# Two transformer layers with routed experts: TensorE's expert pairs written out, and loads and products of the second layer placed beside its attention's end

## The reference, cut to what matters

```python
mp = jnp.split(cond_ctx @ mod_w[layer] + mod_b[layer], N_MOD, axis=-1)
...
xs = xs + ms[2][:, None, :] * ys
...
aff = jax.nn.softmax(jnp.dot(xt, w_router), axis=-1)
g, idx = lax.top_k(aff.T, cap)
xe = xt[idx]
h = jax.nn.silu(xe @ w_gate) * (xe @ w_up)
ye = (h @ w_down) * g[..., None]
out = jnp.zeros_like(xt).at[idx.reshape(-1)].add(ye.reshape(-1, D))
```

## Time and profile before

| | |
|---|---|
| median of 3 runs | 1890.08 us (1889.51 to 1894.63) |
| the profiled execution's own time | 1888.88 us |
| its span in the profile | 1886.9 us |
| TensorE matmul busy | 1660.1 us, 88% of the span |
| VectorE, ScalarE, GpSimd busy | 602.3, 364.8, 312.2 us |
| data moved | 525.07 MB, mean 278 GB/s |
| mean granted TensorE clock | 0.948 |

### The profile page before, as it was taken

One profiled execution on the slowest core, in us unless ns is written; L12 is line 12 of the kernel. 1 busy time (PEld: TensorE's weight loads), 2 busy tenths in 40 slices (PEclk: granted clock), 3 DMA queues, 4 the chain that ended last, 5 costly groups with the idle time before them and its releaser, 6 DMA issues.

```text
span 1886.9 us, 30470 instructions
## 1 busy us (share of the span) xinstructions
PE 1660.1 (88%) x13255; PEld 771.5 (41%) x13255; DVE 602.3 (32%) x1077; ACT 364.8 (19%) x725; POOL 312.2 (17%) x358
## 2 busy tenths in 40 slices
PE   4799868479999999999989788893899999999997
PEld 0688546123332322332258666562233233233322
DVE  2568564510110110120176577535101101210102
ACT  2377731100000000000052365402000000000000
POOL 1133230110101110110020167301101101101110
PEclk8899979789999999999989899896899999999999
DMA  9400642989999999999830201019799999999993
GB/s 391 139 1 1 246 167 112 414 328 407 379 409 375 392 406 371 385 406 413 333 137 1 95 24 33 36 44 417 268 395 391 405 366 388 407 373 391 411 358 116
DMA packets 57682, 525.07 MB, mean 278 GB/s; under 512 B 12351, under 2 KB 12639, under 8 KB 24782
## 3 DMA queue, kind: packets, MB, share of 16 engines
q1 hardware_dynamic: 47968, 490.62, 64.5%
q0 software_dynamic: 8176, 27.08, 5.3%
q10 hardware_dynamic: 1406, 5.38, 0.7%
HBM read 500.50 MB, written 22.55 MB: 277 GB/s over the span
## 4 chain that ended last, share of the span: by engine, by line
PE 77%; DVE 10%; DMA 5%; ACT 4%; issue 3%; POOL 1%; SPq 0%; DVEq 0%; POOLq 0%; ACTq 0%
PE ps L862 36%; PE ps L866 17%; PE ps L813 6%; PE ps L1104 4%; DMA W<-x_hat,gi_c 2%; DMA ring<-in_mod_w 2%; DMA ring<-in_rg_w_in 1%; PE ps L1152 1%; PE ps L1139 1%; PE ps L1126 1%; PE ps L889 1%; PE ps L1024 1%; PE ps L904 1%; ACT W L1332 1%; PE ps L1002 1%
## 5 line engine op out<-in xcount | busy, mean ns | idle before, releaser
L862 PE MATMUL ps<-ring,W 128*32 128x512 f32 x4608 | 558.4, 603 | 19.3 <-issue 18.0
L866 PE MATMUL ps<-ring,W 128*16 128x512 f32 x2304 | 300.6, 594 | 0.0
L862 PEld LDWEIGHTS ps<-ring,W 128*32 128x32 f32 x4608 | 146.8, 111 | 353.3 <-issue 351.1
L1172 ACT ACTIVATE W<-ps 128x512 f32<-128x512 f32 (+5 forms) x129 | 70.3, 562 | 923.1 <-PE ps L904 730.4
L1621 DVE TENSOR_TENSOR W<-ps,amod 128x1024 f32<-128x1024 f32 (+1 forms) x32 | 28.5, 891 | 516.1 <-PE ps L889 394.7
L862 PE MATMUL ps<-over_rows,W 128*32 128x512 f32 x1536 | 182.7, 593 | 0.0
L866 PEld LDWEIGHTS ps<-ring,W 128*16 128x16 f32 x2304 | 68.2, 98 | 179.7 <-issue 179.7
L1630 DVE TENSOR_TENSOR W<-ps,W 128x1024 f32<-128x1024 f32 x16 | 19.6, 1224 | 278.1 <-PE ps L866 278.1
L813 PE MATMUL ps<-wo_hl,mo_hi 128*128 128x512 f32 x320 | 89.2, 402 | 14.6 <-DVE mo_lo L1541 14.6
L866 PE MATMUL ps<-over_rows,W 128*16 128x512 f32 x768 | 100.0, 592 | 0.0
L862 PEld LDWEIGHTS ps<-over_rows,W 128*32 128x32 f32 x1536 | 48.4, 110 | 108.0 <-issue 107.6
(11 more groups left out here) (277 smaller groups left out, 2172.2 us busy)
## 6 DMA issues: line engine op xcount, KB each, us to landing
ring<-in_moe_w_down SPq DMA_DIRECT2D x52, 2048.0 KB, 11.5
ring<-in_moe_w_up SPq DMA_DIRECT2D x48, 2048.0 KB, 13.0
ring<-in_moe_w_gate SPq DMA_DIRECT2D x44, 2048.0 KB, 9.8
ring<-in_mod_w SPq DMA_DIRECT2D x48, 1024.0 KB, 10.7
over_rows<-in_moe_w_gate SPq DMA_DIRECT2D x20, 2048.0 KB, 11.3
over_rows<-in_moe_w_up SPq DMA_DIRECT2D x16, 2048.0 KB, 9.3
over_rows<-in_moe_w_down SPq DMA_DIRECT2D x12, 2048.0 KB, 12.7
ring<-in_rg_w_in SPq DMA_DIRECT2D x8, 1024.0 KB, 27.4
```

The source lines that it names most:

```text
L862: nc.tensor.matmul(ps[q * CG:(q + 1) * CG, bank + n, :], lat(q, k), expert_slots(slots[q // 2], 1)[:, 0, cols], start=(k == 0), stop=(k == ...
L866: mm = nc.tensor.matmul(ps[q * CG:q * CG + CC, bank + 2, :], ctx(a, k), expert_slots(slots[a], 1)[:, 0, h * D + n * 512:h * D + (n + 1) * ...
L1172: nc.scalar.activation(out, in_, ACT.Copy).then_inc(done, n)
```

## The change: what it does

It has three parts.

1. TensorE alone no longer uses `steps`: its 8 pair bodies per layer are written out with constants. SP, POOL, ScalarE and VectorE keep the loop.
2. `modulation(11)` moves from behind `mixer_out(1)` into the attention's loop, behind round NU+1, into bank 0; TensorE waits for ScalarE's copy of it (`mod_row`, 12) before `mixer_out(1)`. ScalarE's copy moves ahead of `mixed_high(1)`.
3. On SP, `first(8)` and `first(10)` of layer 1 now stand ahead of `store_x(1, r2)`, and `row_buffers` (`first(12)`, `first(14)`) gets one more wait: for the first pair's gathered rows.

```diff
         def mod_bank(n):
-            return 0 if n in (3, 4) else 6
+            return 0 if n in (3, 4, 11) else 6
...
                 else:
+                    store_x(1, r2)
                     sp.wait_ge(out_mm, 2 * NT)
                     for n in range(16, 24, 2):
                         first(n)
+
+                    sp.wait_ge(gathered, 32 * NP + 32)
                     row_buffers()
...
             load_mod(11, wo_lo_ok, lambda s: KB + 2 * (s + 1))
-            store_x(1, r2)
             load_moe(1)
...
                 for _ in gate_up(16, at, 3, 0):
                     pass
-                steps(pe, body)
+                for i in range(NP):
+                    body(i, i % 2, i < NP - 1, i < NP - 2)
...
                     mm.then_inc(pv_mm, 1)
+                if i == NU + 1:
+
+                    pe.wait_ge(s_max, 2 * NU)
+                    modulation(11, turn_last=False)
+            pe.wait_ge(mod_row, 12)
             pe.wait_ge(o_ok, NU)
             mixer_out(1, lambda: gate_rows(1, diag1))
             pe.wait_ge(gate_ok, 8)
-            modulation(11, turn_last=False)
             turn(3, 1)
...
+            mod_reads([11], turn_last=False)
             mixed_high(1)
             gate_copy(1, gb1)
             squares(3, 2 * NT)
-            mod_reads([11], turn_last=False)
             store_xhat(1)
```

More of the change, by code:

```diff
@@ L368, in load_mod, with store_x @@
                     put(MOD_SLOT[v] + s, mod_w[v, s])
+            def store_x(layer, x1):
+                sp.wait_ge(x1_ok, 2 * NT * (layer + 1))
+                sp.dma_start(x_res[layer].rearrange("(t p) d -> p t d", p=P), tok(x1)).then_inc(x1_stored, 16)
             def load_moe(layer):
@@ L409, in load_moe @@
                 steps(sp, step_loads)
-            def store_x(layer, x1):
-                sp.wait_ge(x1_ok, 2 * NT * (layer + 1))
-                sp.dma_start(x_res[layer].rearrange("(t p) d -> p t d", p=P), tok(x1)).then_inc(x1_stored, 16)
             sp.dma_start(tok(r2), x_tiles).then_inc(x_in, 16)
```

## The result

The changed kernel takes 1871.41 us (median of 4 runs, 1870.51 to 1872.08), the kernel before 1892.36 us (4 runs, 1889.51 to 1896.25). The ratio is 0.9895, 95% interval 0.9877 to 0.9912: 21 us faster, where 25.1 were forecast. The forecast of 1865.0 us was 6.4 us too low; the time lies in its range of 1860 to 1874. (It was worked out from 1890.08 us for the kernel before, the median of three runs; a fourth run moved that median to 1892.36.)

What follows compares the result with a forecast made beforehand. The prediction took PE to bound the kernel, with a full DMA system beside it. Its terms, -22.8 + 1 + 3.8 - 8.6 + 1.5 = -25.1 us, took 1890.08 to 1865.0 us, range 1860 to 1874.

Steps and rivals of the forecast that it cites:

- Part 1's removal: Experts' loop on PE: writing out the pairs removes four loop returns at a mean of 5.7 us, -22.8 us.
- (C): Rival: the experts' holes are code fetches that straight code needs too, so writing out gains nothing; 1886.8 us, chance 0.04.
- (B): Rival: without pauses the DMA system becomes the bound and PE waits for gathered rows; 1874 us, chance 0.12.
- The +1 us for them: Experts of both layers: gathers get tight once PE's pauses are gone, +1 us, bounds 0 to +10.
- (D): Rival: POOL's two scatters and one gather outgrow the pair's period, making the kernel slower, 1901 us; chance 0.02.
- Part 2's term: Attention's end: moved modulation products and ScalarE's copy lengthen PE's path; +3.8 us net, bounds +2.0 to +7.8.
- half is lost, 1.5 us, if the clock stays up over the short wait: Mixer's output: half of its 3.1 us slow start comes back if the clock stays up, -1.5 us.
- Gain 0: Behind the mixer's output: taking the modulation products away only lengthens PE's wait for VectorE's norm to 8 us, 0 us.
- Part 3's gather: Start of layer 1's experts: first gather takes 4.5 us instead of 13.1, -8.6 us, bounds 0 to -8.6.
- The second pair's rows: Layer 1's experts: the second pair's gather shares the DMA engines with the held loads, +1.5 us, bounds 0 to +3.
- The prediction's reading of the turns that queues take: DMA engines: packet-by-packet turns would at most double the gather to 9 us, gaining 4.5 us; the trace disagrees, 13.1 against 4.5.
- (E): Rival: the attention's end costs its upper bound, 7.8 us, and the first gather gains half; 1873 us, chance 0.10.

Runs made afterwards that it cites:

- the kernel with the loop kept: The changed kernel with TensorE's loop put back, so only the moved products, early loads and hold remain: 1889.26 us against 1889.45 for the kernel before, ratio 0.9999.
- the products in the gap: The changed kernel with `modulation(11)` moved behind the attention's last value products, into PSUM bank 4, and ScalarE's copy behind mixed_high: 1867.05 us.
- part 1 alone: The kernel before with only TensorE's pairs written out, products and loads left where they were: 1871.73 us, ratio 0.9904.
- the hold taken out: The changed kernel without the new wait for the first pair's gathered rows before the last two loads: 1869.0 us, ratio 0.9887.
- the long execution with layer 0 looped: Profiled run of the kernel before with TensorE's pairs written out in layer 1 only: 1884.4 us; median of 6 runs 1878.55 us, ratio 0.9934.
- one hold: The kernel before with pairs written out and the last two loads held for the first pair's gathered rows; products and other loads not moved: 1867.63 us.
- two holds: The kernel before with pairs written out, last two loads held for the first pair's rows, the very last also for the second pair's: 1864.0 us.

## Why the prediction was right, and where it was off

**Part 1's removal was right**, in size and in kind: two returns per layer, each a hole and slow records behind it, 22.8 us forecast and 22.75 measured between the marks. Rival (C) is out, and with it the 0.4 us that come from the figure of about 108 ns for a compare-and-branch in "Advanced Engine Details and Errata" of the Trainium skill ("Control Flow Timing"). So is (B): landings of the loads in the changed kernel lie at 10.9 to 14.9 us in 490 to 556, up from 11.3 to 13.9, and no pair waited for its rows. The +1 us for them was 0. (D) never came near.

**Part 2's term was right for the attention**: 5.3 + 0.55 - 0.6 = 5.25 us forecast, and 5.15 in the kernel with the loop kept, where the clock did not fall in the attention. The step that failed is "half is lost, 1.5 us, if the clock stays up over the short wait". It didn't. PE still waited 2.50 us for `mo_lo`, and the mixer's output met a slow clock a little later: 0.74 from 1202 to 1205, and 12.79 us for its first 48 records, where they had taken 12.66. Nothing of the 1.5 us came. With the products in the gap, where the clock did stay up, they took 11.13: the size was right and the condition failed. The other step that failed is "Gain 0" for the hole they left, which cost up to 0.8 us. The stretch behind it took 14.84 to 14.96 us in three kernels with the products moved and 14.07 in a fourth, 13.87 to 14.42 where they had stayed. From the mixer's output to the router's transposes it is 82.70 us, before 81.70: 1 us lost where 1.5 were booked as gained. So part 2 cost 6.2 us where 3.8 were forecast (5.15 and 1.08 in the kernel with the loop kept).

**Part 3's gather was right**: -8.6 forecast, -8.7 measured. The second pair's rows: +1.5 forecast, the wait was 1.52. What was missed are the 1.37 us of slow products ahead of this wait; the stretch is 2.9 us longer in all. (The forecast's 5.1 us between two loads is a slip: 65.61 / 12 is 5.5. Nothing hangs on it.)

The prediction's reading of the turns that queues take was wrong, and not the rule in "DMA: Bandwidth & Descriptors" of the Trainium skill ("Queues, rings and completion order"). It took one turn each to mean at most twice the time. In the kernel before, while the first pair's gathers went through beside the last loads of weights, 1315 to 1322, SP's queue (q1) and POOL's (q0) moved (packets, MB, share of the 16 engines):

```profile
q1 hardware_dynamic: 164, 2.42, 83.0%
q0 software_dynamic: 156, 0.57, 20.0%
```

That is about one packet of POOL's for each of SP's, and here the trace agrees with the rule. But most packets of the loads carry 16 KB and take 0.61 us, and most of POOL's 4 KB and 0.16 us. So POOL's queue had a fifth of the time, not half. The turns are not all of it: from the issue of the latent rows' gather (1311.26) to the first packet of POOL's it was 4.2 us, where it was 1.8 in the changed kernel, and no run tells why.

**What the sum lacked** is the clock in stretches that the change leaves alone. Some 5.7 us are there: 1.6 and 1.7 in the two pair tails and 2.5 in the attention. The forecast took a stretch without an edit to cost what it did before. The runs show this as the cause and not as a name for the rest: part 1 alone fell short by 5.1 us, its windows show the same three falls, and two products that compute nothing bring 5.6 us back. The terms then close. Measured on the two profiled spans: -22.75 (pairs), +1.55 and +1.70 (tails), +7.99 (attention, with the products), +1.00 (mixer's output to router), -8.71 (to the first rows), +2.88 (to the first pair mark), and -1.65 at the start and in the projection, is -18.0 us, all of the difference between 1886.9 and 1868.9.

Against the forecast's -25.1 this is 7.1 us short: 5.7 for the clock just named, 2.5 from the mixer's output on, 1.4 ahead of the second pair's rows and 0.15 in the terms that came out nearly right, less 1.0 that the gathers did not cost and 1.65 at the start and in the projection, which no term explains. So part of the nearness of the forecast is luck. It is luck too that the time lies in the range: the range reached to 1874 for (B) and (E), and neither happened, while the clock in untouched stretches was no rival. (A slip in the chances changes nothing: (C), at 0.04, lies wholly within 5.7 us of no change, for which 0.03 was given.)

**What stays open** is why the clock falls there. The short waits behind the last pair (1.35, 1.20 and 0.69 us in the changed kernel) are in both kernels alike. In both profiles with two loops it held behind both layers, in nearly all written-out ones it fell, but in "the products in the gap", which is written out, it held behind layer 1 (its tail took 40.1 us, before 40.2). In the attention it held with the hold taken out, though both layers were written out, and fell in the long execution with layer 0 looped. So it may go more with where the waits come in time than with the code of the pairs; no run tests that, and the runs don't tell what decides it.

## What to carry to other kernels

A hole of 3.8 us at a loop's return costs PE 5.7 us, with the slow records behind it; at a round of 137 us and with PE as the bound that is 4% of the loop. A transfer that the critical path waits for should find the DMA queues empty: holding back loads that aren't yet due did that, where making room for them earlier by moving products onto PE's path cost 5.5 us for the same gain. But held loads meet the next gather: one hold won 8.2 us ahead of the first rows and lost 5.6 behind them against part 1 alone, and two holds won 8.8 and lost 1.0. Before work is moved out of a place, look at what PE does there afterwards: here it waited longer and then ran slowly for up to 0.8 us more. And an edit that shifts the program in time can move the clock in stretches that it doesn't touch, so compare those stretches too before a rest is put down to the edit.

## What the runs showed of the hardware that was not expected

- Two products with an unused result, 2.1 us of PE records per layer put into waits of 1.35 and 1.20 us, made a kernel 4.6 us and another 5.6 us faster; the trace shows with them the granted clock at 1.00 behind both layers and, with nothing added there, in the attention too, which is where about half of the gain lies (2.4 and 2.7 us).
- The second gather of the first pair (the context rows) landed 4.4 to 4.9 us after its issue on empty DMA engines, 8.2 us beside one load of 2 MB issued 4.5 us ahead of it, and 13.1 us beside two issued some 4 us ahead of it and the last of an earlier series, though it has a queue of its own. The packets of the two queues went one for one, and most of the loads' were four times as large.
- The last load of 2 MB could be held until 1320.5 and still be in time at 1328.7; alone it landed in 8.2 us.
